# Two ends of an attention stage: the order in which queries and keys are stacked, and where ScalarE makes one minus gate

## The reference

```python
h = rms_norm(x, attn_norm)
proj = h @ w_in                     # 12 parts: NSA q, three k/v pairs, gates; HGRN2 q, f, i, g
y_nsa = rms_norm(nsa_mixer(...))    # 8 query heads, 2 key/value groups, head width 64
y_hg = hgrn2_mixer(hq, hf, hi, hg)  # 4 heads of 128, f = lb + (1 - lb) * sigmoid(.), k = 1 - f
x = x + concat([y_nsa, y_hg]) @ w_out
h = rms_norm(x, mlp_norm)
x = x + square(relu(h @ w_mlp_in)) @ w_mlp_out
```

## Time and profile before

| | us |
|---|---|
| median of 3 runs | 1470.96 |
| lowest and highest | 1465.0, 1474.64 |
| the profiled execution | 1472.83 |
| its span, first to last instruction | 1471.0 |
| its mean granted TensorE clock | 0.992 |

### The profile page before, as it was taken

How to read it: one execution, slowest core, us unless ns; L and a number is a source line. 1 busy time by engine, 2 the same in 40 slices (tenths; PEclk the granted TensorE clock), 3 DMA queues, 4 the chain that set the end, 5 groups by cost and what they waited for, 6 DMA issues and landing times.

```text
span 1471.0 us, 21626 instructions
## 1 busy us (share of the span) xinstructions
PE 1428.5 (97%) x7950; PEld 1222.5 (83%) x7950; DVE 870.2 (59%) x1630; ACT 623.0 (42%) x1235; POOL 161.5 (11%) x178
## 2 busy tenths in 40 slices
PE   7999999999999999998999989999999999999999
PEld 6888888878888888898987868888888788888887
DVE  3002681106666776669784586666666598569764
ACT  5014302215554545460440467755555554444441
POOL 2433343521000000000242000000000000000000
PEclk9999999998999999999999999999999999999999
DMA  5211114200000000012011014444444966643332
GB/s 176 61 47 51 51 36 122 72 7 1 1 2 1 1 2 1 1 44 115 30 51 36 30 36 165 158 152 157 157 158 139 327 206 191 213 127 100 93 115 86
DMA packets 78254, 129.42 MB, mean 88 GB/s; under 512 B 8973, under 2 KB 26826, under 8 KB 78154
## 3 DMA queue, kind: packets, MB, share of 16 engines
q1 hardware_dynamic: 77968, 128.01, 27.3%
q10 hardware_dynamic: 186, 0.08, 0.0%
HBM read 94.51 MB, written 33.55 MB: 87 GB/s over the span
## 4 chain that ended last, share of the span: by engine, by line
PE 87%; DVE 8%; ACT 2%; issue 2%; DMA 1%; SPq 0%; DVEq 0%; ACTq 0%
PE ps L518 64%; PE ps L2102 6%; PE ps L2062 4%; PE ps L2077 4%; PE ps L2122 3%; PE ps L2096 1%; PE ps L2046 1%; PE ps L1935 1%; DVE negmax L1492 1%; PE ps L2067 1%; DMA x_in<-in_x_dram 1%; PE ps L757 1%; DVE q_stack L1485 1%; PE ps L624 0%; DVE hgrn_A L1599 0%
## 5 line engine op out<-in xcount | busy, mean ns | idle before, releaser
L518 PE MATMUL ps<-mlp_w_high,hidden_high 128*128 128x512 f32 x448 | 174.3, 389 | 0.0
L518 PE MATMUL ps<-mlp_w_low,hidden_high 128*128 128x512 f32 x448 | 174.3, 389 | 0.0
L518 PE MATMUL ps<-mlp_w_high,hidden_low 128*128 128x512 f32 x448 | 174.3, 389 | 0.0
L518 PE MATMUL ps<-w_high,hT_high 128*128 128x512 f32 (+1 forms) x448 | 170.5, 380 | 0.8 <-ACT cmp_v L1072 0.7
L518 PE MATMUL ps<-w_low,hT_high 128*128 128x512 f32 (+1 forms) x448 | 168.1, 375 | 0.0
L518 PE MATMUL ps<-w_high,hT_low 128*128 128x512 f32 (+1 forms) x448 | 168.0, 375 | 0.0
L2102 PE MATMUL ps<-nsa,probs_T 128*128 128x64 f32 x1056 | 138.2, 275 | 0.0
L1664 DVE TENSOR_TENSOR mlp_w_low<-mlp_w_raw,mlp_w_high 128x512 fp32r<-128x512 f32 x112 | 77.1, 690 | 98.3 <-ACT mlp_w_high L1200 98.3
L1299 ACT ACTIVATE mlp_w_high<-mlp_w_raw 128x512 fp32r<-128x512 f32 x112 | 70.6, 630 | 148.2 <-PE ps L518 148.2
L2102 PEld LDWEIGHTS ps<-nsa,probs_T 128*128 128x128 f32 x1056 | 129.5, 193 | 0.0
L1744 DVE TENSOR_TENSOR mlp_w_low<-mlp_w_raw,mlp_w_high 128x512 fp32r<-128x512 f32 x112 | 77.0, 688 | 65.8 <-ACT mlp_w_high L1299 65.8
(11 more groups left out here) (234 smaller groups left out, 2893.1 us busy)
## 6 DMA issues: line engine op xcount, KB each, us to landing
hidden_raw<-hidden_pieces SPq DMA_DIRECT2D x112, 256.0 KB, 2.7
mlp_w_raw<-in_w_mlp_in_dram SPq DMA_DIRECT2D x32, 512.0 KB, 4.2
hidden_pieces<-hidden SPq DMA_DIRECT2D x64, 256.0 KB, 2.8
mlp_w_raw<-in_w_mlp_out_dram SPq DMA_DIRECT2D x64, 256.0 KB, 4.3
w_raw<-in_w_in_dram SPq DMA_DIRECT2D x56, 256.0 KB, 2.7
hidden_pieces<-hidden_s SPq DMA_DIRECT2D x48, 256.0 KB, 2.2
x_in<-in_x_dram SPq DMA_DIRECT2D x8, 512.0 KB, 7.3
w_raw<-in_w_out_dram SPq DMA_DIRECT2D x16, 256.0 KB, 2.8
```

The lines of the kernel that those rows point to most:

```text
L518: ins = nc.tensor.matmul(out_ap, a_hl[i], b_hl[j], start=first and n == 0, stop=last and n == 2, skip_group_check=onto_a_sum_already_read)
```

## The change

At the entry the ten stacks are made in another order: slc and win keys of group 0 (m = 0 to 3), then the query head 0 (m = 4, 5, `Q_AT = 4`), then slc and win keys of group 1 (m = 6 to 9). POOL stages in the same order with the same waits, ACT and DVE write each bank to its new place (`STACK_AT`), and PE's first cmp scores wait for 6 subtractions in place of 10. PE still issues all ten stacks ahead of them, and `transposes(0)` still waits for all ten.

At the exit ACT makes `hk` as soon as its own copies are done and the last scores have read the keys whose memory `hk` takes (`qk_done` 136), not behind `o_free` 72; that wait now stands between the table load and the squares. PE, whose first three units need no bank of attention's outputs, waits for `o_free` 72 ahead of the fourth alone.

```diff
--- before.py
+++ after.py
@@ -614,6 +614,9 @@
 
         return tensor[:, m // 4, (m // 2) % 2, (m % 2) * BW:(m % 2 + 1) * BW]
 
+    STACK_AT = (0, 1, 4, 5, None, None, 2, 3, 6, 7)
+    Q_AT = 4
+
     def key_bank(m):
 
         return T_BANK + m % 4
@@ -959,13 +962,10 @@
                 pool.tensor_copy(stage[:, slot, :, :, :], src.unsqueeze(2).to_broadcast([P, NT, 2, DK])).then_inc(stage_ready, 1)
 
             pool.wait_ge(hid_full, 2)
-            for n in range(4):
+            for n, col in enumerate((KS0, KW0, Q0, KS0 + DK, KW0 + DK)):
                 if n >= 2:
                     pool.wait_ge(t_full, 2 * (n - 1))
-                col = (KS0, KW0)[n // 2] + (n % 2) * DK
                 stage_head(n, n % 2, nsa[:, :, col:col + DK])
-            pool.wait_ge(t_full, 6)
-            stage_head(4, 0, nsa[:, :, Q0:Q0 + DK])
             for h in range(1, NH):
                 pool.wait_ge(t_full, FIRST + (it.prep[h - 2][1] + 1 if h > 2 else 0))
                 stand_alone(pool)
@@ -1084,13 +1084,11 @@
                     act.activation(hv[:, i, t, :], ps[:, t, :], func, scale=rstd[:, t:t + 1]).then_inc(proj_out, 1)
 
 
-            for m in range(8):
+            for m in range(FIRST):
                 act.wait_ge(t_full, m + 1)
-                act.activation(key_stack(KS_H, m), ps[:, key_bank(m), :], ACT.Copy).then_inc(t_act, 1)
-
-            for half in range(2):
-                act.wait_ge(t_full, 8 + half + 1)
-                act.activation(QT[:, 0, half * BW:(half + 1) * BW], ps[:, key_bank(8 + half), :], ACT.Copy).then_inc(t_act, 1)
+                half = m - Q_AT
+                to = QT[:, 0, half * BW:(half + 1) * BW] if STACK_AT[m] is None else key_stack(KS_H, STACK_AT[m])
+                act.activation(to, ps[:, key_bank(m), :], ACT.Copy).then_inc(t_act, 1)
 
             def out_act(act, c):
                 act.wait_ge(O_full, c + 1)
@@ -1139,11 +1137,12 @@
 
 
 
-            act.wait_ge(o_free, 72)
+            act.wait_ge(qk_done, len(it.items))
             for n in range(4):
                 act.activation(flat(hk[:, 2 * n:2 * n + 2, :]), fm[:, 1, 2 * n:2 * n + 2, :, :].rearrange("p c h t -> p (c h t)"),
                                ACT.Copy, scale=-1.0, bias=1.0).then_inc(k_done, 1)
             table_for(act, ACT.Ln)
+            act.wait_ge(o_free, 9 * NH)
             for t in range(NT):
                 if t >= 2:
                     act.wait_ge(ysum_ready, t - 1)
@@ -1468,14 +1467,14 @@
                 dve.tensor_scalar(fm[:, 1, :, h, :], fm[:, 1, :, h, :], lb[:, 1, h:h + 1], lb[:, 0, h:h + 1], ALU.mult, ALU.add)
 
 
-            for m in range(8):
+            for m in range(FIRST):
                 dve.wait_ge(t_act, m + 1)
-                dve.tensor_tensor(key_stack(KS_L, m), ps[:, key_bank(m), :], key_stack(KS_H, m).bitcast(F32),
-                                  ALU.subtract).then_inc(t_dve, 1)
-            for half in range(2):
-                dve.wait_ge(t_act, 8 + half + 1)
-                q = QT[DK:P, 0, half * BW:(half + 1) * BW]
-                dve.tensor_tensor(q, ps[DK:P, key_bank(8 + half), :], q.bitcast(F32), ALU.subtract).then_inc(t_dve, 1)
+                if STACK_AT[m] is None:
+                    q = QT[DK:P, 0, (m - Q_AT) * BW:(m - Q_AT + 1) * BW]
+                    dve.tensor_tensor(q, ps[DK:P, key_bank(m), :], q.bitcast(F32), ALU.subtract).then_inc(t_dve, 1)
+                else:
+                    dve.tensor_tensor(key_stack(KS_L, STACK_AT[m]), ps[:, key_bank(m), :], key_stack(KS_H, STACK_AT[m]).bitcast(F32),
+                                      ALU.subtract).then_inc(t_dve, 1)
             at_ = Steps(att_step)
 
             def prep(hh, half):
@@ -1997,17 +1996,13 @@
 
 
             pe.wait_ge(proj_out, 8 * len(blocks))
-            for m in range(8):
+            for m in range(FIRST):
                 n, half = divmod(m, 2)
                 if half == 0:
                     pe.wait_ge(stage_ready, n + 1)
                 if m >= 4:
                     pe.wait_ge(t_dve, m - 3)
                 stack_half(pe, m, n % 2, half, key_bank(m))
-            pe.wait_ge(stage_ready, 5)
-            for half in range(2):
-                pe.wait_ge(t_dve, 5 + half)
-                stack_half(pe, 8 + half, 0, half, key_bank(8 + half))
             pe.wait_ge(m_loaded, 32)
 
             def bank_free(m):
@@ -2038,7 +2033,7 @@
                         pe.wait_ge(o_free, it.items[u][1] * 9 + 1)
                 if kind == "cmp":
 
-                    pe.wait_ge(t_dve, FIRST + (it.groups[it.prep[hh][1]]["dve_after"] if hh else 0))
+                    pe.wait_ge(t_dve, FIRST + it.groups[it.prep[hh][1]]["dve_after"] if hh else Q_AT + 2)
                     nc.tensor.matmul(ps[:, s_, :], masks[:, 0:P], cmask[:], start=True, stop=False, skip_group_check=True)
                     for t in range(NT):
                         o = ps[:, s_, t * NCP:(t + 1) * NCP]
@@ -2124,6 +2119,8 @@
                 return ins
 
             for cp in range(4):
+                if cp == 3:
+                    pe.wait_ge(o_free, 9 * NH)
                 pe.wait_ge(k_done, cp + 1)
                 for c in range(2 * cp, 2 * cp + 2):
                     ins = product(cp, c, lambda h: fm[:, 0, c, h, :])
```

## The result

The changed kernel takes 1462.38 us (median of 11 executions, 1461.57 to 1466.9) against 1472.73 us for the kernel before (11 executions, 1465.0 to 1475.13): a ratio of 0.995, 95% interval 0.9933 to 0.9967, or 10.4 us. Run again later it gave 1462.13 us and 0.9948 (0.9928 to 0.9967). The profiled execution of it took 1464.07 us, 8.8 us less than that of before. The gain is clear of zero and lies within the 1% (14.7 us) that the prediction called no change.

A forecast was written before the change was run, and what follows sets the result against it. PE, busy 97% of the span, was taken as the bound, with two waits each followed by a slow clock. Entry wait 3.28, clock 3.0 and exit 3.40 sum to 9.7 us: forecast 1463 us, range 1457 to 1469.

The forecast's parts named there:

- The entry's wait: Start of attention: first cmp scores start at 334.5, so DVE's maximum starts at 336.62, not 339.90; 3.28 us gained.
- The clock behind it: Behind the first cmp scores: PE's clock no longer falls near 337.0; 3.0 us gained, bounds nothing to 4.13.
- rival A: Both ends: short matmuls, not gaps, lower the clock; gain 5.1 us, 1467.7, or 1466.1 if at entry alone; chance together 0.27.
- The exit: End of attention: earlier `hk`, PE continues without a gap at held clock; 3.40 us gained, bounds 1.85 to 4.1.
- The sum: Whole kernel: 3.28 + 3.0 + 3.40 = 9.7 us gained, from the profiled 1472.83 to 1463.1 us.
- a new low stretch appeared elsewhere: Anywhere else in the kernel: a sign, given without size, that would show the prediction wrong.
- Setting the median: Whole kernel: the profiled execution lies 1.9 us above the median of before; this was not taken off the forecast again.
- B: Both ends: waits only change places; entry gives at most 1.96 us, exit nothing, 1470.8 us; chance 0.08.
- C: Levels behind the exit: shifted bursts lose the clock, 2.0 us each, slower from five bursts on; chance 0.03.

The follow-up runs named there:

- the order alone: The kernel before with the new order of stacks, first cmp scores still waiting for all ten subtractions, exit as before: 1471.67 us, ratio 0.9999.
- the filled gap: At the entry: the kernel before plus 15 unread identity transposes behind the ten stacks, scores still waiting for the tenth subtraction: 1468.36 us, ratio 0.9974.
- the exit alone: The kernel before with only the exit's three edits, entry as before: 1470.63 us, ratio 0.9988.
- the filled exit gap: The kernel before plus 14 unread identity transposes behind attention's last outputs, filling PE's 1.85 us gap: 1472.03 us, ratio 1.0006.

## Why the prediction was right

**The entry's wait.** 3.28 us were predicted for the way to the maximum. It came at 336.74 on a scale shifted by 0.15: 3.31 us. The ten subtractions end 7.65 us behind the first transposes, 7.53 before, so they kept their pace to 0.1 us, and the order alone gave 0.9999.

**The clock behind it.** 3.0 us were predicted, between 0 and 4.13; the rest of the 6.9 us of E is 3.6. Less of PE's saving went into waits than I took; the cost of it is visible as 0.6 us more idle time ahead of the first transposes. That the gap and not the short matmuls brought the clock down, which decided between forecast and rival A, is shown by the filled gap, 4.9 us at E, and by the count over all profiles, four falls in four with the gap.

**The exit.** 3.40 us predicted, 3.51 measured; the units begin right behind the outputs, the first doubling comes 10.30 us behind `hq`'s start where 10.4 were forecast. The split was not asked for: 1.6 of it are the clock (filled gap, X 12.2 us; by the profile alone, as the time of that run didn't show it), 1.9 the earlier start, of which 0.8 hang on PE's moved wait.

**The sum.** 9.7 predicted, 10.4 at the first doubling. What the sum lacked was the fall at 767 us, 1.6 us in the profiled execution, which left 8.8: I had written that the prediction would be wrong if a new low stretch appeared elsewhere, but gave it no term. It comes in some executions and not in others: four of the 14 profiles have it, with 1.4 to 1.7 us more behind the levels. One of them, the exit alone, has the old entry. All four have the changed exit (four of nine such profiles, none of the five with the old exit); whether that is chance no run settles. The median hardly feels it: 1462.38 us, against 1461.87 for an execution whose profile lacks it.

**Setting the median.** I didn't take the 1.9 us between the profiled execution and the median of three off the forecast, because an execution of before that missed a fall would owe its speed to clock terms which the kernel after doesn't have. With 11 executions the median of before is 1472.73 us, 0.1 from the profiled one, so there was nothing to take off. That a forecast built on one execution of a kernel that scatters by 10 us landed 0.6 us from the median is partly luck; the terms themselves, 3.31, 3.6 and 3.51 us, are not. The reason given is supported too. The executions of before range from 1464.5 us at a mean clock of 0.996 to 1476.4 at 0.989; those of the changed kernel from 1461.2 to 1466.9. Where the clock is 0.997 in both, the distance is about 3 us (1464.8 and 1461.8), not far from the 1.9 + 1.9 us of the two waits without clock terms; where before has 0.989, it is 13. That these clusters are executions with neither and with both falls is argued from their mean clock; none of before at 0.989 or 0.997 was profiled.

**The rivals.** A is out at the entry by time and profile, at the exit by the profiles: the filled gap there gave full clock but no time. The Trainium skill's "TensorE: Matmul & The Clock Gate", section "HAM oscillation — how this bites in real kernels", warns only of longer gaps, and here falls follow gaps of 1.96, 1.85 and 2.05 us, and filling the first removed the fall behind it: page and measurement differ, and the measurement decides. What Part 1 of that page says of a monitor that runs free of the kernel agrees with the gap of 2.05 us in the `w_out` stage, which costs the clock in four profiles and not in the ten others. B is out: X shows DVE ready 0.66 us ahead of PE. C occurred in its smallest form, one fall of 3.4 us in the levels of four profiles, with the price of nothing that its own text gave for a single burst.

## What to carry to other kernels

Look for short idle times of TensorE that stand ahead of stretches at half clock: here two gaps of 3.8 us together cost another 6.5 us by the clock behind them (4.9 and 1.6 in the profiles), and closing them by letting the next products wait for no more than they read was worth more than the waits themselves. Check first, by filling the gap with products that nobody reads, whether the stretch behind it is TensorE's to speed up. Where DVE and ACT set the pace, as ahead of the tenth product of the MLP here, a held clock gives next to nothing, and the fall may come a few us later where it costs more. And a before whose executions scatter by 10 us with the mean clock needs many executions, or distances within profiles, to show 3 us.

## What the runs showed that was not expected

Extra work made the kernel faster: 15 transposes whose result nobody reads, 1472.5 to 1468.4 us. At the entry the clock stayed low for 13.7 us in one execution, 17.1 in another and 6.8 in a third of the same code with the same gap, with PE busy all the time; matmuls of 64 columns, each with a weight load, fill much of that stretch. At the exit, ahead of matmuls of 128 columns, it came back after 3.4 us in most profiles and 6.8 in one. And with a delay of 0.8 us of the first scores about half of the executions were 4 us slower or more. The one such execution that was profiled, with the first gap filled, has its fall at a later gap that was there all along. That finding has no cause yet, and neither has the filled exit gap, which gave 1.6 us in its profile and nothing in the median.
